# Expert weights loaded in 8 KB runs, with the gate and up products taken by quarters of the rows

## The chip, the cores and the metric

The kernel runs on one core of a Trainium2 chip. The metric is the device time of one launch in microseconds (us). Engines: PE (TensorE), DVE (VectorE), ACT (ScalarE), POOL (GpSimd), SP (SyncE, which here only issues DMAs).

## The reference

One layer of a hybrid backbone over 2048 tokens of 1024 channels. A first sub-layer (a projection, two state mixers, the product with `w_out`) takes the first 1100 us and more and is not touched, apart from its last stage. The second sub-layer is a mixture of 32 experts; each token goes to 2 of them:

```
x = x + g1 * rmsnorm(y, norm_post_mix)
h = rmsnorm(x, norm_pre_ffn) * (1.0 + sc2) + sh2        # the second norm
lg, le = h @ w_rg + b_rg, h @ w_re + b_re               # router: group, then 2 of its 8 experts
for each expert e, for each block of 128 of its (token, weight) pairs:
    xb  = h[tok]
    hid = silu(xb @ w_gate[e]) * (xb @ w_up[e])         # 1024 -> 512
    yb  = hid @ w_down[e]                               # 512 -> 1024
    out[tok] += yb * weight
x = x + g2 * rmsnorm(out, norm_post_ffn)
```

All is float32, and the products carry the float32 precision by splitting each operand into a high part (rounded to the PE's fp32r format) and a low part (the rest): high x high, high x low and low x high are added up.

## The kernel before

Stages follow each other: projection, mixers, **residual** (1111 to 1387 us of the trace), **experts** (1387 to about 2284) and the combining of the rows (to the end). Every engine runs its own program, written out by hand; semaphores tie them together.

**Residual.** It runs over 16 tiles of 128 tokens. For each, PE multiplies with `w_out`, DVE and ACT form the residual `r_x`, DVE forms the second norm `r_h` (also `h2`) in two operations (L2257 times the scale, L2259 plus the shift), PE transposes `r_h` (L2101) for the router's product, and a DMA stores it in DRAM (`second_norm`), where the experts' blocks gather their rows. The eight transposes take the channels k*128 to k*128+127, so the router's weights lie with channel k*128+p on partition p.

**Experts.** `over_blocks` loops over the experts and, within one, over its blocks (48 in all). The last block of an expert has `following`, the number of the next expert: in it the weights of the next expert are also converted. There are 31 such blocks. A block's body, by engine:

- PE: 48 gate and up products into `pG` (two halves of 256 gate and 256 up columns, in PSUM tile `r_py`; L2513 and L2514 high parts of x by both weight parts, L2517 the low part), two transposes of each half of the hidden rows (`turn_h`, L2501), eight transposes of the next block's rows (`turn_x`, L2494), and 24 products with w_down (L2522), 82 in all.
- ACT: silu of half 0 (L2578, into `e_sg`), the copy that makes the high parts of third 0 of the next weights (`high`, L2573: two operations, a sixth each), silu of half 1, the high part of `e_hT` (L2585) and `e_xT` (L2566), `high` of third 1, the output copy `e_y` (L2593, which waits until the scatter of the block before has left the buffer), `high` of third 2.
- DVE: `e_hid` (L2628) of each half, the low parts of `e_hT`, `e_xT` and of the weights (`low`, L2619, two operations a third, each behind its high sixth), its half of `e_y` (L2640).
- SP: loads `e_w_whole`, the raw weights, a third (2 MB) at a time; each third has one buffer, and its load waits until both low sixths of the same third of the expert before are made. Thirds 0 and 1 are columns 0 to 255 and 256 to 511 of w_gate and w_up, in runs of 256 floats (1 KB); third 2 is w_down in runs of 4 KB. So half h of the products needs third h only.
- POOL: gathers the rows of the next block (`e_x`) and scatters and adds the output of the block before (`rows_summed`, L2444), both through the DMA queue q0; the weight loads go through q1. Both carry rows of 1024 floats, one a packet.

`e_w_high` and `e_w_low` are single too: a sixth of the next expert may be written only when the products of this expert that read it are done. In third 0 that is when half 0's 24 products are (`prodG` of half 0).

## Time and profile before

| | |
|---|---|
| median of 3 runs | 2333.85 us (2333.26 to 2334.17) |
| the profiled execution | 2337.66 us, span 2336.0 us |
| experts' 48 blocks | 1386.8 to 2284.1 us |
| mean granted PE clock | 0.969 of full speed |
| DMA traffic | 518.11 MB, mean 222 GB/s |
| products on PE | 11618 instructions |

Busy times are shares of the whole span, over stages with different limits. What bounds the experts is read block by block: a block's length is the distance between the first gate product of one and of the next. In what follows "at 5.6" means 5.6 us after that first product, where a block is spoken of.

### The profile page before, as it was taken

What the parts mean: (1) busy time and instruction counts of PE and PEld (TensorE: products, weight loads), DVE (VectorE), ACT (ScalarE), POOL (GpSimd) and SP (SyncE); (2) the same over time, 40 slices, a digit from 0 to 9 for tenths busy, and PEclk for the clock granted to TensorE, in tenths of its full rate; (3) what the DMA queues carried; (4) which work ended last, traced back from release to release, by engine and by line L of the source; (5) the groups of instructions that cost most, each with busy time, mean ns of one, the idle gap of its engine ahead of it and who ended that gap; (6) DMA issues with size and microseconds to landing.
All of it is one profiled execution on the core that took longest, in us unless ns stands there. A gap on an engine that the chain in (4) does not pass through costs nothing. (4 is left out here: it accounts for less than half of the span.)

```text
span 2336.0 us, 35426 instructions
## 1 busy us (share of the span) xinstructions
PE 2177.8 (93%) x11618; PEld 1836.8 (79%) x11619; DVE 1400.3 (60%) x2033; ACT 1055.3 (45%) x1518; POOL 643.1 (28%) x648
## 2 busy tenths in 40 slices
PE   8999999999999679998999979999999999999990
PEld 5888888899999568887788858778788888887770
DVE  6322222377555578887566665765767675647776
ACT  4422332243223026665333234755666665547763
POOL 0000000000000558887222232221333333323333
PEclk9999999999999889999999989999999999999995
DMA  8632333546551987765554335998988887868997
GB/s 308 237 108 109 127 142 139 187 158 214 175 175 54 333 331 240 233 220 203 160 214 150 118 124 168 344 285 256 338 263 268 270 276 244 252 174 278 350 347 302
DMA packets 297436, 518.11 MB, mean 222 GB/s; under 512 B 33492, under 2 KB 206108, under 8 KB 292584
## 3 DMA queue, kind: packets, MB, share of 16 engines
q1 hardware_dynamic: 271000, 439.52, 55.1%
q0 software_dynamic: 17136, 43.92, 8.4%
q10 hardware_dynamic: 9216, 33.56, 3.5%
q8 instruction: 51, 0.84, 0.2%
q14 instruction: 33, 0.27, 0.0%
HBM read 397.28 MB, written 128.57 MB: 225 GB/s over the span
## 5 line engine op out<-in xcount | busy, mean ns | idle before, releaser
L2619 DVE TENSOR_TENSOR e_w_low<-e_w_whole,e_w_high 128x2048 fp32r<-128x2048 f32 x192 | 431.1, 2287 | 90.6 <-ACT e_w_high L2573 87.1
L2573 ACT ACTIVATE e_w_high<-e_w_whole 128x2048 fp32r<-128x2048 f32 x190 | 353.9, 1914 | 30.2 <-DMA e_w_whole<-in_moe_w_down_dram 18.5
L2513 PE MATMUL r_py<-e_w_high,e_xT 128*128 128x512 f32 x768 | 298.9, 389 | 1.2 <-ACT e_xT L2566 1.2
L2514 PE MATMUL r_py<-e_w_low,e_xT 128*128 128x512 f32 x768 | 298.8, 389 | 0.0
L897 PE MATMUL proj_acc<-w_high,hT_high 128*128 128x512 f32 x672 | 263.9, 393 | 0.3 <-DVE hT_low L1010 0.3
L897 PE MATMUL proj_acc<-w_low,hT_high 128*128 128x512 f32 x672 | 262.0, 390 | 0.0
L897 PE MATMUL proj_acc<-w_high,hT_low 128*128 128x512 f32 x672 | 261.7, 389 | 0.0
L2522 PE MATMUL r_py<-e_w_high,e_hT 128*128 128x512 f32 x768 | 226.7, 407 | 18.0 <-ACT e_hT L2585 17.9
L2517 PE MATMUL r_py<-e_w_high,e_xT 128*128 128x512 f32 x768 | 189.9, 389 | 0.0
L2522 PEld LDWEIGHTS r_py<-e_w_high,e_hT 128*128 128x128 f32 x768 | 138.6, 191 | 45.8 <-ACT e_hT L2585 20.6
L2513 PEld LDWEIGHTS r_py<-e_w_high,e_xT 128*128 128x128 f32 x768 | 144.2, 188 | 31.3 <-issue 1.4
L2517 PEld LDWEIGHTS r_py<-e_w_high,e_xT 128*128 128x128 f32 x768 | 144.2, 188 | 29.9
L2514 PEld LDWEIGHTS r_py<-e_w_low,e_xT 128*128 128x128 f32 x768 | 144.2, 188 | 29.9
L887 PE MATMUL proj_acc<-hT_high,w_high 128*128 128x256 f32 x576 | 164.4, 285 | 0.0
L887 PE MATMUL proj_acc<-hT_low,w_high 128*128 128x256 f32 x576 | 164.1, 285 | 0.0
L887 PE MATMUL proj_acc<-hT_high,w_low 128*128 128x256 f32 x576 | 164.0, 285 | 0.0
L1230 DVE SCALAR_TENSOR_TENSOR conv_out<-ch,cw,conv_out 128x258 f32<-128x258 f32 x288 | 119.4, 480 | 72.3 <-ACT conv_out L805 72.2
L897 PEld LDWEIGHTS proj_acc<-w_high,hT_high 128*128 128x128 f32 x672 | 126.5, 188 | 29.5 <-issue 3.5
L897 PEld LDWEIGHTS proj_acc<-w_high,hT_low 128*128 128x128 f32 x672 | 126.3, 188 | 26.5
L897 PEld LDWEIGHTS proj_acc<-w_low,hT_high 128*128 128x128 f32 x672 | 126.4, 188 | 24.9
L2049 PE MATMUL r_py<-r_w_high,r_yT 128*128 128x512 f32 x512 | 142.1, 394 | 0.0
L2423 POOL COPY e_rows_held<-e_rows_held 128x6 int32<-128x6 int32 x48 | 32.2, 672 | 360.6 <-issue 253.1
(311 smaller groups left out, 4196.2 us busy)
## 6 DMA issues: line engine op xcount, KB each, us to landing
e_w_whole<-in_moe_w_gate_dram SPq DMA_DIRECT2D x64, 1024.0 KB
e_w_whole<-in_moe_w_up_dram SPq DMA_DIRECT2D x64, 1024.0 KB
e_w_whole<-in_moe_w_down_dram SPq DMA_DIRECT2D x64, 1024.0 KB
by_token<-tok SPq DMA_DIRECT2D x32, 512.0 KB, 3.0
w_in_raw<-in_w_mod_dram SPq DMA_DIRECT2D x32, 512.0 KB, 4.4
m_tok<-by_token SPq DMA_DIRECT2D x16, 768.0 KB, 5.5
s_kv<-by_token SPq DMA_DIRECT2D x20, 512.0 KB, 5.9
modulated_high<-hT_high SPq DMA_DIRECT2D x9, 1024.0 KB, 3.9
```

The source lines that it names most:

```text
L887: m = nc.tensor.matmul(bank[:, b * 2 * P:(b + 1) * 2 * P], a[:, PLACE[c], k, w], h[:, s, k], start=(k == 0 and n == 0), stop=(k == KD - 1 ...
L897: m = nc.tensor.matmul(bank, h[:, s, k, span], (wh if high_ else wl)[:, PLACE[c], k], start=(k == 0 and n == 0), stop=(k == KD - 1 and n = ...
L1230: V.scalar_tensor_tensor(out=v[:, c], in0=chb[:, c, k:k + OUT], scalar=cw[:, k, c:c + 1], in1=v[:, c], op0=ALU.mult, op1=ALU.add).then_inc ...
L2049: m = nc.tensor.matmul(py[:, s, n], yT[:, s, part, k], with_[:, k, n * 512:(n + 1) * 512], start=(k == 0 and part == 0 and with_ is wh), s ...
L2423: nc.gpsimd.tensor_copy(held[:, 0:2], held[:, 1:3]).then_inc(held_on.sem, 1)
L2513: nc.tensor.matmul(pG[:, half], xT[:, 0, k], wh[:, half, w], start=(k == 0), stop=False)
L2514: nc.tensor.matmul(pG[:, half], xT[:, 0, k], wl[:, half, w], start=False, stop=False)
L2517: m = nc.tensor.matmul(pG[:, half], xT[:, 1, k], wh[:, half, k * 512:(k + 1) * 512], start=False, stop=(k == KD - 1))
L2522: m = nc.tensor.matmul(pY[:, n], hT[:, part, k], with_[:, 2, c0:c0 + 512], start=first, stop=last)
L2573: nc.scalar.activation(wh[:, third, part], raw[:, third, part], ACT.Copy).then_inc(whs.sem, 1)
L2619: nc.vector.tensor_tensor(wl[:, third, part], raw[:, third, part], wh[:, third, part].bitcast(F32), ALU.subtract).then_inc(wls.sem, 1)
```

## The change

1. **Loads.** Partition p now receives rows 8p to 8p+7 of w_gate and w_up, whole rows of 512 floats. Third 0 is the first four of these rows of both matrices, third 1 the last four: runs of four neighbouring rows, 8 KB. w_down stays as it was. The router's weights are loaded in the same order of rows.
2. **Second norm.** For the products to match, channel 8q+k of `r_h` is stored at position k*128+q. DVE's two operations (now L2264, L2266) run over 128 x 128 x 8 elements; the output (and the first input of the second) has a stride of 512 bytes between neighbouring elements.
3. **Converted weights.** `e_w_high` and `e_w_low` keep gate and up columns of a half side by side, so a sixth is written in runs of 256 floats (`sixth_of`), and read in whole.
4. **Products.** Both halves now need both thirds. PE takes the first four row chunks for both halves (24 products, then the new counter `rows_done`), then the last four for half 0 (12 products, `prodG` of half 0) and half 1 (12, `prodG` of half 1).
5. **Order on ACT and DVE.** In a block with `following`, ACT waits for third 0 of the next weights and for `rows_done`, makes the first high sixth, and only then silu of half 0; the second sixth stays between the silus. DVE makes the first low sixth ahead of `e_hid` of half 0.

```diff
+def by_chunks(v):
+    return v.rearrange("p (k q) -> p q k", k=KD)
+
+
+def by_rows(v):
+    return v.rearrange("p (q k) -> p q k", k=KD)
...
@@ residual: sync @@
-        sp.dma_start(wr[:, :, 0:NG], io["moe_w_rg"].rearrange("o (k p) n -> p (o k) n", p=P)).then_inc(one, 16)
+        sp.dma_start(wr[:, :, 0:NG], io["moe_w_rg"].rearrange("o (p k) n -> p (o k) n", k=KD)).then_inc(one, 16)
...
@@ residual: vector @@
-                nc.vector.scalar_tensor_tensor(out=h2[:, 1 - s], in0=x1[:, 1 - s], scalar=ss[:, 3:4], in1=g["mod"][:, 2], op0=ALU.mult, op1=ALU.mult).then_inc(h2m.sem, 1)
+                nc.vector.scalar_tensor_tensor(out=by_chunks(h2[:, 1 - s]), in0=by_rows(x1[:, 1 - s]), scalar=ss[:, 3:4], in1=by_rows(g["mod"][:, 2]), op0=ALU.mult, op1=ALU.mult).then_inc(h2m.sem, 1)
                 dve.wait_ge(h2m.sem, h2m.at(t - 1))
-                nc.vector.tensor_tensor(h2[:, 1 - s], h2[:, 1 - s], g["mod"][:, 1], ALU.add).then_inc(h2s.sem, 1)
+                nc.vector.tensor_tensor(by_chunks(h2[:, 1 - s]), by_chunks(h2[:, 1 - s]), by_rows(g["mod"][:, 1]), ALU.add).then_inc(h2s.sem, 1)
...
@@ load_sixth @@
     if third < 2:
-        to = raw[:, third].rearrange("p (k n f) -> p k n f", k=KD, n=2)[:, :, n]
-        eng.dma_start(to, io[src][0, bass.ds(e, 1), :, third * 256:(third + 1) * 256].rearrange("o (k p) f -> p (o k) f", p=P)).then_inc(landed, 16)
+        rows = KD // 2
+        to = raw[:, third, n * THIRD // 2:(n + 1) * THIRD // 2].rearrange("p (k f) -> p k f", k=rows)
+        eng.dma_start(to, io[src][0, bass.ds(e, 1)].rearrange("o (p k) f -> p (o k) f", k=KD)[:, third * rows:(third + 1) * rows]).then_inc(landed, 16)
...
+def sixth_of(buf, third, n, whole):
+
+    if third == 2 or whole:
+        part = buf[:, third, n * THIRD // 2:(n + 1) * THIRD // 2]
+        return part.rearrange("p (j f) -> p j f", f=256) if third < 2 else part
+    return buf[:, third].rearrange("p (j n f) -> p j n f", n=2, f=256)[:, :, n]
...
@@ experts: tensor, body @@
+            def gate_up(half, part, rows):
+                for k in range(4):
+                    w = slice((2 * k + half) * 512, (2 * k + half + 1) * 512)
+                    if part == 0:
+                        nc.tensor.matmul(pG[:, half], xT[:, 0, 4 * rows + k], wh[:, rows, w], start=(rows == 0 and k == 0), stop=False)
+                        nc.tensor.matmul(pG[:, half], xT[:, 0, 4 * rows + k], wl[:, rows, w], start=False, stop=False)
+                    else:
+                        m = nc.tensor.matmul(pG[:, half], xT[:, 1, 4 * rows + k], wh[:, rows, w], start=False, stop=(rows == 1 and k == 3))
+                        if k == 3:
+                            return m
+
+            pe.wait_ge(xTs.sem, xTs.at(b))
+            pe.wait_ge(wls.sem, wls.at(expert_of[0], 2))
             for half in range(2):
...
+                gate_up(half, 0, 0)
+            pe.wait_ge(xTl.sem, xTl.at(b))
+            for half in range(2):
+                m = gate_up(half, 1, 0)
+            m.then_inc(rows_done.sem, 1)
+            pe.wait_ge(wls.sem, wls.at(expert_of[0], 4))
+            for half in range(2):
+                gate_up(half, 0, 1)
+                gate_up(half, 1, 1).then_inc(prodG.sem, 1)
...
@@ experts: scalar, body @@
         def body(b, row, following):
+            if following is not None:
+                act.wait_ge(w_in.sem(0), w_in.at(following))
+                act.wait_ge(rows_done.sem, rows_done.at(b))
+                high_sixth(0, 0)
             for half in range(2):
                 act.wait_ge(prodG.sem, prodG.at(b, half + 1))
                 nc.scalar.activation(sg[:, half], pG[:, half, 0], ACT.Silu).then_inc(sgs.sem, 1)
                 if following is not None and half == 0:
-
-                    high(following, 0)
+                    high_sixth(0, 1)
...
@@ experts: vector, body @@
         def body(b, row, following):
+            if following is not None:
+                low_sixth(following, 0, 0)
             for half in range(2):
...
                 if following is not None and half == 0:
-                    low(following, 0)
+                    low_sixth(following, 0, 1)
```

ACT's program in a block with `following`, before the change, from the top of the body to the output copy (ISA and REGISTER_ALU rows carry waits and addresses; `e_sg` is the silu's output, `r_py` the PSUM tile of the products):

```order
L2578 ACT_TABLE_LOAD
L2578 ACTIVATE e_sg<-r_py 128x256
L2570 ISA
L2573 ACTIVATE e_w_high<-e_w_whole 128x2048 x2
L2577 REGISTER_ALU
L2578 ACTIVATE e_sg<-r_py 128x256
L2584 REGISTER_ALU
L2585 ACTIVATE e_hT<-r_pl 128x256
L2563 REGISTER_ALU
L2566 ACTIVATE e_xT<-r_pT 128x1024
```

The same place of ACT's program after the change:

```order
L2607 ISA
L2608 REGISTER_ALU
L2597 ACT_TABLE_LOAD
L2597 ACTIVATE e_w_high<-e_w_whole 128x8x256
L2611 ISA
L2612 ACT_TABLE_LOAD
L2612 ACTIVATE e_sg<-r_py 128x256
L2597 ACTIVATE e_w_high<-e_w_whole 128x8x256
L2611 REGISTER_ALU
L2612 ACTIVATE e_sg<-r_py 128x256
L2618 ACTIVATE e_hT<-r_pl 128x256
```

One of the two weight copies has moved ahead of the first silu, behind two waits, and there are two table loads in the body where there was one.

DVE's program at the same place, before the change:

```order
L2628 SCALAR_TENSOR_TENSOR e_hid<-e_sg,e_rows_held,r_py 128x256
L2618 ISA
L2619 TENSOR_TENSOR e_w_low<-e_w_whole,e_w_high 128x2048
L2618 REGISTER_ALU
L2619 TENSOR_TENSOR e_w_low<-e_w_whole,e_w_high 128x2048
L2623 REGISTER_ALU
```

And after it:

```order
L2648 ISA
L2649 TENSOR_TENSOR e_w_low<-e_w_whole,e_w_high 128x8x256
L2660 ISA
L2661 ISA
L2664 REGISTER_ALU
L2665 SCALAR_TENSOR_TENSOR e_hid<-e_sg,e_rows_held,r_py 128x256
L2648 REGISTER_ALU
L2649 TENSOR_TENSOR e_w_low<-e_w_whole,e_w_high 128x8x256
```

One subtraction of the next weights now stands ahead of `e_hid` of half 0.

## Rows read from the trace of the kernel before

**Rows 1.** The page: span, busy time of each engine, the two groups that convert weights
```profile
PE 2177.8 (93%) x11618; PEld 1836.8 (79%) x11619; DVE 1400.3 (60%) x2033; ACT 1055.3 (45%) x1518; POOL 643.1 (28%) x648
...
L2619 DVE TENSOR_TENSOR e_w_low<-e_w_whole,e_w_high 128x2048 fp32r<-128x2048 f32 x192 | 431.1, 2287 | 90.6 <-ACT e_w_high L2573 87.1
L2573 ACT ACTIVATE e_w_high<-e_w_whole 128x2048 fp32r<-128x2048 f32 x190 | 353.9, 1914 | 30.2 <-DMA e_w_whole<-in_moe_w_down_dram 18.5
```

**Rows 2.** Windows over stretches of blocks: stretch, length, busy times, PEclk, DMA share, GB/s
```profile
1464.30:1526.80 62.50, 54.94 (x253) 43.93 (x252) 49.41 (x37) 44.64 (x40) 17.75 (x15) 1.00 1.07 347
1526.80:1650.80 124.00, 124.00 (x590) 103.19 (x589) 78.40 (x67) 74.27 (x74) 33.23 (x35) 1.00 0.86 271
1650.80:1672.50 21.70, 19.49 (x85) 15.87 (x84) 16.71 (x13) 15.01 (x14) 6.78 (x5) 0.92 1.07 342
1672.50:2134.80 462.30, 461.65 (x2185) 382.91 (x2184) 290.09 (x247) 275.23 (x273) 144.71 (x130) 1.00 0.82 252
2134.80:2259.10 124.30, 112.28 (x506) 90.42 (x505) 99.66 (x73) 90.41 (x79) 42.48 (x30) 0.97 1.07 348
```

**Rows 3.** Waits over 1420 to 2295: engine, line, releaser, total, times, longest
```profile
ACT e_y L2593 <- DMA rows_summed<-e_y,e_rows_held: 61.0, 16, 6.7
...
ACT e_w_high L2573 <- DMA e_w_whole<-in_moe_w_down_dram: 18.5, 9, 3.1
PE r_py L2522 <- ACT e_hT L2585: 17.9, 10, 2.2
```

**Rows 4.** Timeline of POOL before the block that starts at 1650.8
```profile
1643.12 2.31 POOL L2444 DMA_INDIRECT rows_summed<-e_y,e_rows_held  x1 [0.38 <-issue]
```

**Rows 5.** Timeline of ACT in that block (start, duration, ..., idle before, releaser)
```profile
1653.67 0.60 ACT L2593 ACTIVATE e_y<-r_py 128x512 f32<-128x512 f32 x1 [2.36 <-DMA rows_summed<-e_y,e_rows_held]
1654.16 3.72 ACT L2573 ACTIVATE e_w_high<-e_w_whole 128x2048 fp32r<-128x2048 f32 x2
1657.90 1.28 ACT L2578 ACT_TABLE_LOAD   x1
...
1660.80 3.71 ACT L2573 ACTIVATE e_w_high<-e_w_whole 128x2048 fp32r<-128x2048 f32 x2 [1.22 <-DMA e_w_whole<-in_moe_w_up_dram]
1664.42 0.37 ACT L2578 ACTIVATE e_sg<-r_py 128x256 f32<-128x256 f32 x1
```

**Rows 6.** Timeline of PE in that block: the first products with w_down
```profile
1665.11 1.22 PE L2522 MATMUL r_py<-e_w_high,e_hT 128*128 128x512 f32 x2 [2.21 <-ACT e_hT L2585]
```

**Rows 7.** Windows of full DMA: a store in 8 KB runs, then loads in 4 KB runs
```profile
110.00:115.00 5.00, 5.00 (x25) 4.08 (x24) 0.00 (x0) 0.16 (x2) 0.00 (x0) 1.00 1.02 418
...
2300.00:2320.00 20.00, 0.00 (x0) 0.00 (x0) 20.00 (x19) 12.26 (x22) 13.57 (x13) 0.50 1.03 410
```

**Rows 8.** DMA queues over 1482 to 1484, both with work (q0: gather or scatter)
```profile
q0 software_dynamic: 74, 0.30, 75.6%
q1 hardware_dynamic: 75, 0.25, 33.6%
```

**Rows 9.** Timeline of ACT in an undisturbed block that starts at 1579.9
```profile
1585.57 0.38 ACT L2578 ACTIVATE e_sg<-r_py 128x256 f32<-128x256 f32 x1 [3.46 <-PE r_py L2517]
...
1591.02 0.38 ACT L2578 ACTIVATE e_sg<-r_py 128x256 f32<-128x256 f32 x1 [1.44 <-PE r_py L2517]
```

**Rows 10.** Timeline of DVE in the residual stage: the second norm's last operation
```profile
1330.08 1.23 DVE L2259 TENSOR_TENSOR r_h<-r_h,mod 128x1024 f32<-128x1024 f32 x1
```

**Rows 11.** Timeline of PE: its transposes of tile r_h, one tile and the last
```profile
1333.04 0.71 PE L2101 MATMUL r_pT<-ident,r_h 128*128 128x128 f32 x5
...
1357.21 0.98 PE L2101 MATMUL r_pT<-ident,r_h 128*128 128x128 f32 x7 [1.59 <-DVE r_h L2259]
```

**Rows 12.** Groups of small DVE operations by form: busy time, mean ns of one
```profile
L2235 DVE TENSOR_REDUCE o_sl<-o_wr 128x2 f32<-128x64 f32 x16 | 3.5, 220 | 0.5
L2206 DVE TENSOR_REDUCE o_s<-o_w 128x8 f32<-128x32 f32 x16 | 3.4, 211 | 0.5
...
L2193 DVE TENSOR_TENSOR o_l<-r_pl,r_br 128x4 f32<-128x4 f32 x16 | 2.5, 155 | 0.1
```

More of the change, by code:

```diff
@@ L2566, in xT_copy, with high_sixth @@
             nc.scalar.activation(xT[:, 0], pX[:], ACT.Copy).then_inc(xTs.sem, 1)
+        def high_sixth(third, n):
+            nc.scalar.activation(sixth_of(wh, third, n, False), sixth_of(raw, third, n, True), ACT.Copy).then_inc(whs.sem, 1)
         def high(e, third):
@@ L2571, in high @@
             for n in range(2):
-                part = slice(n * HALF, (n + 1) * HALF)
-                nc.scalar.activation(wh[:, third, part], raw[:, third, part], ACT.Copy).then_inc(whs.sem, 1)
+                high_sixth(third, n)
         def body(b, row, following):
+            if following is not None:
+                act.wait_ge(w_in.sem(0), w_in.at(following))
+                act.wait_ge(rows_done.sem, rows_done.at(b))
+                high_sixth(0, 0)
             for half in range(2):
```

25 lines of the change are left out of this document (8 added, 17 removed).

## The prediction

> **What bounds the kernel now.** I read the page first: PE is busy for 93% of the span, so it sets the time wherever nothing else is late [rows 1]. In the experts I then cut the trace at the first gate product of each block. The windows show two kinds. Seven undisturbed blocks take 124.0 us, 17.7 each, with PE busy throughout [rows 2]. Ten blocks take 62.5 (three), 21.7 (one) and 124.3 us (six), together 208.5 where 177 would do: 31.5 us lost. They are the blocks with `following` that come directly after another such block (experts of one block in a row), so that six thirds of weights, 12 MB, are wanted within two blocks. There the DMA share is 1.07 at 342 to 348 GB/s; in the calm ones it is 0.86 or 0.82 [rows 2]. In the 26 blocks from 1672.5 on, 462.3 us against 460.2, little is lost.
>
> The waits name what ends last in a lost stretch: PE's w_down products wait for ACT's high part of `e_hT`, 10 times, 17.9 us; behind that stands ACT, which has waited for the scatter of the previous output (61.0 us in 16 waits) and for the down third (18.5) [rows 3]. The block at 1650.8 shows the chain. POOL issued the scatter at 1643.12 [rows 4]; it lets ACT copy `e_y` only at 1653.67, frame 2.9 (us after the block's first product). Then come the high copy of the down third to 7.9, a table load of 1.28 us, silu 0, a wait for third 0 to 10.0, its two copies to 13.7, and silu 1 [rows 5]. `e_hT` follows, and PE starts down at 14.3 after 2.21 us idle [rows 6], where a calm block starts it at 11.9. So ACT's order and the DMA queue share the blame.
>
> **The loads: what they give.** The thirds of w_gate and w_up move at about 349 GB/s now, 2.10 MB in 6.0 us [rows 2]. A store in 8 KB runs ran at 418, loads in 4 KB runs at 410 [rows 7]. No row shows 8 KB loads; the bounds are 349 (nothing) and 418, and I take 410 to 418: 5.1 us. A run block's DMA sum was 2 x 6.0 + 5.1 for down + some 3.65 for gather and scatter = 20.8, which is the observed mean (20.85). It becomes 18.9. Upper bound of the gain: 10 x 2.0 = 20 us.
>
> The two queues share an engine packet by packet: while both had work, q0 sent 74 and q1 75 [rows 8]. Beside a 1 KB packet q0 therefore fared well; beside an 8 KB one it waits longer for each turn. An estimate: a 4 KB packet of q0 takes 75.6% of 2 us on 16 engines, over 74 packets, 327 ns [rows 8]; one of 8 KB at 418 GB/s takes 16 x 8192 B / 418 GB/s = 0.31 us. At a share of 1.07 a pair takes 0.59 us, and the scatter's 8 packets an engine 4.75 us instead of about 3.4. Bounds for the `e_y` copy: 0 to 1.3 us later. I take 0.7, since part of the scatter falls where q1 pauses.
>
> **ACT's new order.** A calm block is the measure: silus at 5.7 and 11.1 [rows 9], 24 products apart, 0.227 us each. Now `rows_done` comes with product 24 (5.6), `prodG` of half 0 with product 36 (8.4), of half 1 with 48 (11.1). ACT does high sixth 1.91 us, a second table load of 1.28 (the order shows two in every body with `following`), silu 0, the other sixth 1.91, silu 1; DVE 2.29 a sixth [rows 1].
> - Isolated following block (14): high 5.65 to 7.55, load to 8.85, silu 0 to 9.2, high to 11.1, silu 1 at 11.1; DVE's low 7.55 to 9.85, `e_hid`, low 11.1 to 13.35, `e_hid` 1 to 13.8, so the last low part of `e_hT` comes at 14.05 when PE wants it at 14.0. +0.1 each: +1.4. The cover is thin: whatever delays the first sixth by x costs x.
> - The first of a run (7), in which the down third's copies spill into the frame as well: +0.4 each, bounds 0 and 1.2: +2.8.
> - The second of a run (3; now 20.45 to 21.75, mean 21.0): `e_y` at 3.6, high of down 4.2 to 7.9, load to 9.2, first sixth to 11.1, second load to 12.4, silu 0, `e_hid` behind a low that ends at 13.4, hence `turn_h` at 13.8. But ACT's second sixth and silu 1 stand ahead of the `e_hT` copy, so down starts at about 15.3, against 14.3 before. Add 5.8 for 24 down products, and 1.2 for the slower clock after an idle PE (0.92 over this block now [rows 2]): 22.3. +1.3 each: +3.9.
> - Later ones of a run (7): if a block takes T, the next `e_y` copy moves by 11.7 - T against the start of the down third, and the block's silu by 20.6 - T. It settles at T = 20.4, ACT-bound, where DMA alone would allow 18.9. Now about 20.8. -0.4 each: -2.8.
>
> The wait for third 0 now stands ahead of silu 0, and with it everything behind it on ACT: both silus, `e_hT`, `e_xT`. It lands at 10.0 in the block shown [rows 5]; with loads 2 us quicker a block, at about 8.2, before ACT is free at 9.2. I cost it at nothing for that cover. SP's load of third 0 is issued about 1 us later, since the second low ends later (13.4 for 12.5); that lies within the same 1 us of room. Queued behind it on SP are only the loads of thirds 1 and 2.
>
> PE has the same 48 products; the waits for third 1's low now hold at product 25, as before, and the low part of x at product 17. Nothing. The write in runs of 256 floats is costed at nothing: each run is 1 KB long. Third 2's load, POOL's code, the combine stage: untouched.
>
> **The second norm.** The strided operations are not in the trace. The nearest rows: a reduction that reads 32 elements at a stride of 32 bytes takes 211 ns, one that reads 64 in a row 220, and an operation on 4 elements 155 [rows 12]. From the last two, 1.08 ns an element on top of 151; the strided one has 1.88. So +0.8 ns an element, 0.82 us an operation of 1024, 1.6 us a tile. In a middle tile L2259 ends at 1331.31 [rows 10] and PE's transposes start at 1333.04 [rows 11]: 1.73 us of room, which hides it. In the last tile they start at the operation's end [rows 11], so 1.6 us go to the path. Bounds: 0 (no penalty) and 2 or 3 times the element time.
>
> The Trainium skill bears on this (SBUF — State Buffer, Specifications): lines of 16 bytes, at least two accesses a line wanted for full bandwidth, a penalty at each new line. By it the 512-byte stride is slow for every element. The rows agree in direction (1.7 times), though at 32 bytes; how large it is at 512 no row here shows.
>
> **The sum**, against the profiled 2337.66: +1.4 +2.8 +3.9 -2.8 +1.6 = +6.9; one block of the 26 has already lost about 0.8 that shorter transfers return: +6.1, so 2343.8. The profiled run stands 3.8 us above the median of the runs (2333.85), so the forecast is **2340**.
>
> **The rivals.**
> - *A, the forecast:* ACT's order, the second table load and the later scatter eat the shorter transfers. Bounds of the terms: 2335 to 2346. Chance 0.43.
> - *B, faster:* the `e_y` copy comes earlier, not later, because the queue as a whole empties sooner (share falls below 1.0 between thirds). Then the run blocks follow the DMA sum: 208.5 to 188.5, -20; with +4.2, -0.8 and +1.6 that is -15: 2319, and 2314 if the first terms vanish. For it: 61.0 us of waits for the scatter [rows 3], a saturated queue in all ten blocks [rows 2]. Against: ACT's chain from `e_y` to `e_hT` is 11 us long without any wait. It decides where the `e_y` copy stands: at frame 2.0 or earlier B wins, from 3 on A. Chance 0.25.
> - *C:* A, and the strided operations take twice the element time or more: +1.1 us each, 2.2 a tile, 0.5 beyond the room in 12 tiles (6) and 2.2 in the last: +8.2 for +1.6, 2346.6; 2345 to 2353. Chance 0.17.
> - *D, the loads are no faster:* third 0 then lands at 10 to 11 and holds silu 0 back; 1.5 us more in ten blocks, +15 on A, 2355. Rows 7 speak against it. Chance 0.05.
> - *E, nothing to see:* B by half, 2330 to 2338. Chance 0.10.
>
> The Trainium skill (DMA: Bandwidth & Descriptors, Specifications) puts the least transfer for line rate at 512 B, by which 1 KB runs would already be at full rate and D would hold. The trace disagrees: 347 against 410 GB/s at a share above 1.0 in both [rows 2, 7].
>
> **How the numbers follow.** 0.2%, 4.7 us, is about what a measurement of this kernel can tell from no change: "same" reaches from 2329.2 to 2338.5. A puts about 0.14 below 2338.5 and 0.29 above. Faster: B and a bit of E, 0.27. Same: 0.14 of A, E's rest, a remainder: 0.25. Slower: A 0.29, C 0.17, D with what lies beyond: 0.48. The range has to take in most of B and C: 2314 to 2353; A's own is 2335 to 2346.
>
> **What would show it.** After: thirds 0 and 1 in run blocks at about 410 GB/s; two table loads in each following body; silu 0 at 8.9 in isolated following blocks and PE without a gap there; the second blocks of runs at about 22, later ones at about 20.4; PE's wait for `e_hT` larger in the second ones. L2264 and L2266 at about 2.1 us. Wrong if run blocks come near 19 (B), if the residual's period of a tile grows (C), if ACT waits for third 0 ahead of silu 0 (D), or if the PE idles in isolated following blocks, which I hold to be just covered: 14 blocks there turn each 0.3 us of mistake into 4.

## The result and the profile after

The changed kernel takes 2371.65 us (median of 4 runs, 2364.44 to 2381.62), the kernel before 2334.01 in the same comparison: a ratio of 1.0152, 95% interval 1.0123 to 1.0181. It is 36 us slower by that ratio (38 by the medians) where 6 were forecast, outside the range. Its runs also scatter over 17 us, those of before over 5. The profiled execution of the changed kernel (2381.62 us, span 2380.0) is the slowest of the four, so its stretches sum up to 44 us more than before, not to 36.

First the page of the changed kernel: busy times, then the two groups that convert weights.

```profile
PE 2198.4 (92%) x11618; PEld 1847.2 (78%) x11619; DVE 1426.0 (60%) x2033; ACT 1096.6 (46%) x1549; POOL 667.2 (28%) x648
...
L2649 DVE TENSOR_TENSOR e_w_low<-e_w_whole,e_w_high 128x2048 fp32r<-128x2048 f32 x192 | 433.4, 2288 | 164.1 <-ACT e_w_high L2597 164.1
L2597 ACT ACTIVATE e_w_high<-e_w_whole 128x2048 fp32r<-128x2048 f32 x190 | 357.0, 1915 | 32.1 <-PE r_py L2529 31.8
```

The durations of one operation are those of [rows 1] (2288 for 2287 ns, 1915 for 1914). Nothing has become slower by itself in these two; the time is in waiting. The first gate product of each block divides the experts again. The windows below are the run blocks of [rows 2] (three, one and six), two other blocks (1589.7 and 1744.3), and three microseconds in which only a load of gate and up ran (1732 to 1735):

```profile
1474.20:1536.30 62.10, 55.28 (x253) 43.87 (x252) 50.27 (x37) 49.40 (x43) 18.53 (x15) 1.00 1.00 358
...
1589.70:1607.60 17.90, 17.90 (x85) 14.65 (x84) 9.17 (x9) 12.52 (x12) 7.31 (x5) 1.00 0.60 212
1664.10:1690.50 26.40, 19.30 (x86) 16.00 (x85) 16.87 (x13) 16.36 (x15) 7.39 (x6) 0.87 0.85 282
1744.30:1768.00 23.70, 19.50 (x86) 15.89 (x85) 11.18 (x10) 8.35 (x10) 8.71 (x6) 0.93 0.83 269
1732.00:1735.00 3.00, 3.00 (x15) 2.47 (x14) 3.00 (x3) 2.98 (x2) 2.78 (x2) 1.00 1.02 429
2177.30:2302.10 124.80, 114.31 (x505) 92.54 (x504) 100.38 (x73) 98.39 (x85) 38.51 (x30) 0.95 0.96 344
```

What the reader is to see: the ten run blocks lose little more than before (62.1 for 62.5; 26.4 for 21.7; 124.8 for 124.3; together 213.3 for 208.5). But blocks that lost nothing before are now long. The one at 1744.3 takes 23.7 us; the one at 1589.7 still takes 17.9, but the block behind it 20.4. There are five such blocks (numbers 11, 18, 21, 24, 31, counted from 0). None of them has `following` itself; each comes directly behind one or two blocks that have. They were 17.7 us each before and now take 20.4, 23.7, 21.9, 22.8 and 22.1: 22.4 us lost in blocks that no step of the prediction speaks of. The DMA share is 0.83 to 1.00 in the slow stretches, where it was 1.07 in the run blocks before; and a load in 8 KB runs goes at 429 GB/s.

The waits over the experts, to be held against [rows 3]:

```profile
ACT e_y L2626 <- DMA rows_summed<-e_y,e_rows_held: 107.8, 26, 7.4
...
PE r_pl L2518 <- DVE e_hid L2665: 40.8, 14, 7.1
...
ACT L2597 <- DMA e_w_whole<-in_moe_w_up_dram: 10.0, 10, 1.8
```

ACT's output copy waits 107.8 us for the scatter in 26 places (61.0 in 16 before). PE now waits for the hidden rows. Number 17 and its successor show the whole chain. First POOL in the changed kernel, where block 17 starts at 1726.1, then in the kernel before, where it starts at 1707.9:

```profile
1732.05 2.28 POOL L2440 COPY e_rows_held<-e_rows_held 128x6 int32<-128x6 int32 x1 [9.57 <-issue]
1734.49 2.03 POOL L2445 COPY e_rows_held<-e_ids 128x3 int32<-128x3 int32 x1 [0.17 <-POOL e_rows_held L2440]
...
1738.27 2.97 POOL L2461 DMA_INDIRECT rows_summed<-e_y,e_rows_held  x1 [0.38 <-issue]
```

```profile
1712.88 1.15 POOL L2423 COPY e_rows_held<-e_rows_held 128x6 int32<-128x6 int32 x1 [8.60 <-issue]
1714.20 2.03 POOL L2428 COPY e_rows_held<-e_ids 128x3 int32<-128x3 int32 x1 [0.16 <-POOL e_rows_held L2423]
...
1717.97 2.32 POOL L2444 DMA_INDIRECT rows_summed<-e_y,e_rows_held  x1 [0.38 <-issue]
```

The scatter is issued at frame 12.2 instead of 10.1, and takes 2.97 us to be issued instead of 2.32. The first copy starts 1.0 us later in the block, and the two small copies together take 4.3 us (3.2 before); they take 0.2 us each where nothing holds them. Beside them, DVE of the changed kernel:

```profile
1729.80 6.68 DVE L2649 TENSOR_TENSOR e_w_low<-e_w_whole,e_w_high 128x2048 fp32r<-128x2048 f32 x3
```

Three subtractions in a row, 2.2 us apart, from 1729.80 to 1736.5. POOL's first copy ends at 1734.33, where the second of them ends; its second copy ends at 1736.52, with the third. The scatter's data then land so late that ACT, which may not overwrite `e_y` before, stands for 7.33 us. First ACT's copy in the kernel before, in block 18, which starts there at 1725.6; then ACT, DVE and PE in block 18 of the changed kernel, which starts at 1744.3:

```profile
1728.70 0.60 ACT L2593 ACTIVATE e_y<-r_py 128x512 f32<-128x512 f32 x1 [2.54 <-DMA rows_summed<-e_y,e_rows_held]
```

```profile
1752.04 0.60 ACT L2626 ACTIVATE e_y<-r_py 128x512 f32<-128x512 f32 x1 [7.33 <-DMA rows_summed<-e_y,e_rows_held]
1752.54 3.71 ACT L2597 ACTIVATE e_w_high<-e_w_whole 128x2048 fp32r<-128x2048 f32 x2
1756.26 1.28 ACT L2612 ACT_TABLE_LOAD   x1
1757.56 0.66 ACT L2612 ACTIVATE e_sg<-r_py 128x256 f32<-128x256 f32 x2
```

```profile
1758.89 0.87 DVE L2665 SCALAR_TENSOR_TENSOR e_hid<-e_sg,e_rows_held,r_py 128x256 f32<-128x256 f32 x2
```

```profile
1759.50 0.43 PE L2518 MATMUL r_pl<-ident,e_hid 128*128 128x128 f32 x2 [4.20 <-DVE e_hid L2665]
```

The output copy comes at frame 7.8 for 3.1 before. Behind it on ACT stand the two high sixths of the down third, a table load and the silus; DVE's hidden rows come behind its last low sixth; and PE, which wants them at the end of its 48 products, waits 4.20 us. At frame 3.1 the same row of work ended in time. In the five blocks the output copy comes 3.5 to 5.7 us later than before.

The packets' records of the two traces show where the time goes in block 17. The scatter is issued 2.1 us later and its issue takes 0.65 us longer; its 128 packets, of 327 ns each in both, are spread over 6.2 us instead of 3.9. What releases POOL's first copy stands in the kernel: POOL's loop waits until the scatter and the gather of the block before have landed. A late gather thus hands the lateness on. Before block 10, the gather lands 2.7 us later in its block than it did, POOL's first copy starts at frame 7.3 for 4.6, and the scatter is issued at 11.7 for 6.9.

Last, the second norm's two operations, and the two DMA queues in two microseconds of block 18 in which both had work:

```profile
L2264 DVE SCALAR_TENSOR_TENSOR r_h<-r_x,r_ss,mod 128x1024 f32<-128x1024 f32 x16 | 33.1, 2071 | 0.6 <-POOL r_ss L254 0.6
...
L2266 DVE TENSOR_TENSOR r_h<-r_h,mod 128x1024 f32<-128x1024 f32 x16 | 32.0, 2003 | 0.5
```

```profile
q0 software_dynamic: 53, 0.22, 55.1%
q1 hardware_dynamic: 50, 0.39, 50.9%
```

They take 2071 and 2003 ns, 0.79 and 0.78 us more than before. The queues still take turns packet by packet (53 to 50), as in [rows 8], and where a load in 8 KB runs is the neighbour each turn lets 8 KB of it pass ahead of 4 KB of q0.

### The profile page after: what moved, and what is told of

The parts are those of the page before. It is cut to its first block and busy times, and to the rows that moved or that the text cites. A ratio compares the mean times of both kernels' runs of the same rounds, so it can differ in the third digit from the quotient of the medians.

```text
span 2380.0 us, 35440 instructions
## 1 busy us (share of the span) xinstructions
PE 2198.4 (92%) x11618; PEld 1847.2 (78%) x11619; DVE 1426.0 (60%) x2033; ACT 1096.6 (46%) x1549; POOL 667.2 (28%) x648
## 5 line engine op out<-in xcount | busy, mean ns | idle before, releaser
L2649 DVE TENSOR_TENSOR e_w_low<-e_w_whole,e_w_high 128x2048 fp32r<-128x2048 f32 x192 | 433.4, 2288 | 164.1 <-ACT e_w_high L2597 164.1
L2597 ACT ACTIVATE e_w_high<-e_w_whole 128x2048 fp32r<-128x2048 f32 x190 | 357.0, 1915 | 32.1 <-PE r_py L2529 31.8
L2526 PE MATMUL r_py<-e_w_high,e_xT 128*128 128x512 f32 x768 | 298.9, 389 | 1.3 <-ACT e_xT L2594 1.3
L2529 PE MATMUL r_py<-e_w_high,e_xT 128*128 128x512 f32 x768 | 197.6, 389 | 0.0
L2440 POOL COPY e_rows_held<-e_rows_held 128x6 int32<-128x6 int32 x48 | 37.0, 772 | 385.5 <-issue 265.0
```

The source lines that it names most:

```text
L2440: nc.gpsimd.tensor_copy(held[:, 0:2], held[:, 1:3]).then_inc(held_on.sem, 1)
L2526: nc.tensor.matmul(pG[:, half], xT[:, 0, 4 * rows + k], wh[:, rows, w], start=(rows == 0 and k == 0), stop=False)
L2529: m = nc.tensor.matmul(pG[:, half], xT[:, 1, 4 * rows + k], wh[:, rows, w], start=False, stop=(rows == 1 and k == 3))
L2597: nc.scalar.activation(sixth_of(wh, third, n, False), sixth_of(raw, third, n, True), ACT.Copy).then_inc(whs.sem, 1)
L2649: nc.vector.tensor_tensor(sixth_of(wl, third, n, False), sixth_of(raw, third, n, True), sixth_of(wh, third, n, False).bitcast(F32), ALU.su ...
```

## The experiments

Fourteen kernels, each timed in five rounds against the kernel before. "Order" is the new order on ACT and DVE. Ratios are to the kernel before.

| kernel | median us | ratio, 95% interval |
|---|---|---|
| order_alone | 2359.93 | 1.0105 (1.0091 to 1.0120) |
| small_runs | 2356.16 | 1.0080 (1.0067 to 1.0093) |
| plain_norm | 2372.09 | 1.0172 (1.0140 to 1.0205) |
| early_scatter_after | 2443.65 | 1.0460 (1.0447 to 1.0474) |
| dve_rows_after | 2343.74 | 1.0028 (1.0019 to 1.0037) |
| dve_rows_before | 2332.35 | 0.9978 (0.9969 to 0.9987) |
| old_order | 2369.65 | 1.0155 (1.0139 to 1.0171) |
| strided_turn | 2378.69 | 1.0170 (1.0145 to 1.0195) |
| one_table | 2365.06 | 1.0119 (1.0101 to 1.0137) |
| all_edits | 2324.02 | 0.9948 (0.9935 to 0.9961) |
| all_edits_2k | 2325.77 | 0.9956 (0.9942 to 0.9970) |
| split_lows | 2366.61 | 1.0134 (1.0104 to 1.0164) |
| all_edits_1k | 2337.80 | 1.0000 (0.9991 to 1.0009) |
| order_rows | 2348.14 | 1.0044 (1.0030 to 1.0058) |

**order_alone: the order without the loads.** On the kernel before:

```diff
         def body(b, row, following):
+            if following is not None:
+                act.wait_ge(w_in.sem(0), w_in.at(following))
+                act.wait_ge(prodG.sem, prodG.at(b, 1))
+                high_sixth(0, 0)
...
-                    high(following, 0)
+                    high_sixth(0, 1)
```

and likewise on DVE, one low sixth ahead of the hidden rows.

> The kernel before (1 KB runs, products by halves, plain second norm) with the new order of ACT and DVE alone: the first high sixth ahead of silu 0, the first low sixth ahead of the hidden rows. Theory ORDER (three subtractions in a row on DVE hold up POOL's small copies, so the scatter is issued 2 us later and the output copy waits): most of the loss is here, 20 to 30 us slower than before, with the blocks after a pair of following blocks at 20 us or more. Theory PACKETS (the scatter's 4 KB packets wait behind 8 KB ones): at most 8 us slower, what the hand schedule gave (+1.4, +2.8, +3.9), and those blocks stay at 17.7.

Measured: 23 us slower, but not where the theory ORDER said. The five blocks (11, 18, 21, 24, 31) stay at 17.7; the first and second blocks of a run grow (the seven first ones take 136.3 us together for 125.3, the three second ones 68.6 for 63.0). The waits:

```profile
ACT L2576 <- DMA e_w_whole<-in_moe_w_up_dram: 32.2, 17, 3.2
...
ACT e_y L2599 <- DMA rows_summed<-e_y,e_rows_held: 4.4, 4, 1.4
```

ACT no longer waits for the scatter (4.4 us); it waits for third 0, 32.2 us in 17 places. In block 17 of that kernel:

```profile
1721.80 1.28 ACT L2576 ACT_TABLE_LOAD   x1 [1.01 <-DMA e_w_whole<-in_moe_w_up_dram]
1723.09 1.92 ACT L2576 ACTIVATE e_w_high<-e_w_whole 128x2048 fp32r<-128x2048 f32 x1
1725.02 1.28 ACT L2585 ACT_TABLE_LOAD   x1
```

Third 0 lands 5.5 us into the block, later than ACT would take it; then come a table load, a sixth, and the second table load, all ahead of silu 0. ACT had been free since 4.5. The prediction had costed this wait at nothing, since it put its landing in a run at 8.2 and ACT's readiness at 9.2; it had not looked at the first blocks of runs, and in this kernel ACT waits in the second and later ones too (23.7 of the 32.2 us). So in its time ORDER was right (20 to 30 us), in its mechanism wrong.

**small_runs: the change with 1 KB packets.**

```diff
-        to = raw[:, third, n * THIRD // 2:(n + 1) * THIRD // 2].rearrange("p (k f) -> p k f", k=rows)
-        eng.dma_start(to, ...rearrange("o (p k) f -> p (o k) f", k=KD)[:, third * rows:(third + 1) * rows])
+        to = sixth_of(raw, third, n, False)
+        eng.dma_start(to, ...rearrange("o (p k) (h f) -> p (o k h) f", k=KD, h=2)[:, 2 * third * rows:2 * (third + 1) * rows])
...
-    if third == 2 or whole:
+    if third == 2:
```

> The changed kernel, but the eight rows of a partition are written into the raw buffer in runs of 1 KB, so that the packets are as small as before; rows, products, order and the strided norm are those of the change. PACKETS: 2340 to 2348, the late output copies gone. ORDER: 2362 or more, or slower still, since the transfers lose their speed too. If both act: in between, near 2355.

Measured: 2356, "in between", 15 us faster than with 8 KB packets. Again the same two waits:

```profile
ACT L2597 <- DMA e_w_whole<-in_moe_w_up_dram: 31.5, 17, 3.0
...
ACT e_y L2626 <- DMA rows_summed<-e_y,e_rows_held: 10.5, 6, 4.8
```

With 1 KB packets third 0 is late (31.5 us) and the scatter is not (10.5). With 8 KB packets it is the other way round: 10.0 and 107.8. The long runs shorten the one wait and lengthen the other by more. The blocks show it too. With 1 KB packets, though POOL's copies and the order are those of the change, the five blocks are back at 17.7 us (22.3 us less in all), while the seven first blocks of runs take 5.5 us more. So it takes 8 KB packets to make the five blocks long.

**plain_norm and strided_turn: the strided operations.** plain_norm stores the second norm as before (the router's weights too; the expert products pair channels with other rows). strided_turn does the same and mends the products on PE:

```diff
-                m = nc.tensor.transpose(pX[:, k], xb[:, k * P:(k + 1) * P], ident)
+                m = nc.tensor.transpose(pX[:, k], xb[:].rearrange("p (q k) -> p k q", k=KD)[:, k], ident)
```

> The changed kernel with the second norm's two operations unstrided and the router's weights in the old order of rows (so the tokens go to the same experts; the expert products then pair channels with the wrong rows of the weights, values only). Both theories: the residual stage shortens by about 5 us (1391.7 to 1386.8 at the first gate product), the rest stays: 5 us faster than the changed kernel.

> The changed kernel with the second norm stored plainly, and PE's eight transposes of a block's rows reading every eighth channel instead (a stride of 32 bytes). If PE reads strided rows at its usual pace the 5 us of the residual stage come back (first gate product at 1386 to 1388 for 1391.7) and the rest stays: 5 us faster than the changed kernel. If a strided read doubles a transpose (0.27 to 0.5 us), 8 x 0.25 x 48 = up to 90 us slower.

Measured: neither is faster in the median (2372 and 2379, with runs from 2366 to 2392). The effect is seen inside the stage only: from PE's first transpose of `r_y` to the first gate product it takes 275.5 us before, 278.2 in the changed kernel, 275.5 in plain_norm and 276.3 in strided_turn. So the strided norm costs some 2.6 us; in all traces of this document the stage takes 277.5 to 278.6 us with it and 275.2 to 276.3 without. The rest of the 4.9 by which the experts begin later lies ahead of this stage, in code that is not touched: the stage starts anywhere between 1106.7 and 1113.5 us in these traces. In the experts more than this differs from trace to trace: the five blocks take 110.9 us in the trace of the changed kernel, 96.7 in plain_norm, 101.9 in strided_turn. PE's strided transposes take 300 ns on average in strided_turn against 285 for the plain ones of plain_norm, and 278 with the same stride in all_edits below; plain ones take 273 to 307 in the other traces. A stride of 32 bytes costs PE nothing that can be told from this spread.

**early_scatter_after: the scatter ahead of the second copy.**

```diff
             shift(b)
+            scatter(b)
             take(b)
...
             pool.dma_start(ids[:], dram["ids"][bass.ds(row, P), :]).then_inc(ids_in.sem(0), 16)
-            scatter(b)
```

> The changed kernel, but POOL issues the scatter directly behind its first small copy, ahead of the second copy and of the load of the next row numbers: about 4 us earlier in the block. ORDER: takes back more than the 2 us that the copies lose, so 25 us or more faster than the changed kernel, 2345 or less. PACKETS: the scatter still crawls at 6 us beside the 8 KB loads, but starts earlier: 10 to 20 us faster, 2350 to 2360. The output copies' waits for the scatter (107.8 us in the changed kernel) fall accordingly.

Measured: 72 us slower than the changed kernel. A clear miss; neither theory had this. The waits say why:

```profile
POOL e_x L2451 <- DMA e_ids<-tokens_sorted: 272.8, 41, 9.5
...
DVE e_hid L2665 <- POOL e_rows_held L2440: 67.9, 22, 5.0
```

The load of the next row numbers goes through the same queue q0 as the scatter, and now stands behind its 128 packets: POOL waits 272.8 us for it (90.5 in the changed kernel), the gather and the next block's first copy are late, and DVE's hidden rows wait for that copy (67.9 us).

**dve_rows_after and dve_rows_before: POOL's copies on DVE.** Both on top of their kernels:

```diff
 gpsimd:
-            shift(b)
-            take(b)
             pool.wait_ge(taken.sem, taken.at(b))
 vector, behind its half of the output copy:
+            nc.vector.tensor_copy(held[:, 0], held[:, 1]).then_inc(moved.sem, 1)
+            ...
+            nc.vector.tensor_copy(held[:, 1], held[:, 2]).then_inc(held_on.sem, 1)
+            ...
+            nc.vector.tensor_copy(held[:, 2], ids[:]).then_inc(taken.sem, 1)
```

> The changed kernel, but the three small copies of row numbers that POOL made ahead of each scatter are made by DVE, right behind its half of the output copy. Theory PORT (in the changed kernel a gather that lands 1.6 us later beside 8 KB packets pushes POOL's two copies into DVE's row of back-to-back subtractions, each copy ends only with a subtraction, and the scatter is issued 4 to 5 us later): the scatters are issued at frame 1 to 6, the blocks 11, 18, 21, 24 and 31 fall back to about 18, and 15 to 25 us of the loss go: 2345 to 2357. Rival SLOW PACKETS ALONE (the scatter crawls beside 8 KB packets wherever it stands): those blocks stay above 19.5, no more than 8 us gained.

> The same edit on the kernel before. PORT: output copies that wait for the scatter (61.0 us in 16 waits) come earlier; the ten run blocks are bound by DMA all the same, so 0 to 10 us faster than before, unless the 0.6 us of small copies on DVE, which is busy nearly throughout in following blocks, cost more. SLOW PACKETS ALONE: no change or slower by up to 10.

Measured: 28 us faster than the changed kernel, 1.0028 of the kernel before. Blocks 11, 18, 21, 24 and 31 are back at 17.7 us. POOL in block 17, which starts at 1714.4 there, and the two waits:

```profile
1720.80 0.58 POOL L2474 DMA_DIRECT2D e_ids<-tokens_sorted  x1 [10.01 <-issue]
1721.76 2.93 POOL L2462 DMA_INDIRECT rows_summed<-e_y,e_rows_held  x1 [0.38 <-issue]
```

```profile
ACT L2593 <- DMA e_w_whole<-in_moe_w_up_dram: 12.5, 10, 1.9
...
ACT e_y L2622 <- DMA rows_summed<-e_y,e_rows_held: 5.9, 4, 3.8
```

The scatter is issued at frame 7.4 for 12.2, though it still takes 2.93 us to issue and its packets still take turns with 8 KB ones. ACT's wait for it falls from 107.8 to 5.9 us. So slow packets alone do not make the loss; the late issue is needed. With small_runs this makes two conditions: take away the 8 KB packets or POOL's copies, and the five blocks are 17.7 us again. On the kernel before, the same edit brings some 5 us (0.9978).

**split_lows: shorter operations on DVE.**

```diff
-            nc.vector.tensor_tensor(low, raw, high, ALU.subtract).then_inc(wls.sem, 1)
+            nc.vector.tensor_tensor(low[half[0]], raw[half[0]], high[half[0]], ALU.subtract)
+            nc.vector.tensor_tensor(low[half[1]], raw[half[1]], high[half[1]], ALU.subtract).then_inc(wls.sem, 1)
```

> The changed kernel with each subtraction of weights on DVE cut in two halves, nothing else. PORT (a copy on POOL is held until the DVE operation running beside it ends): POOL's copies, up to 2.3 us long in the changed kernel, are now at most 1.2 us, the scatters are issued 1 to 2 us earlier, and 5 to 15 us of the loss come back although DVE has more instructions. If POOL's copies are slow for another reason, they stay at up to 2.3 us, and the time is that of the changed kernel or a few us more for 192 more operations.

Measured: 2366.6, 5 us faster than the changed kernel, less than the scatter of its runs (2360.6 to 2386.9): inconclusive as a time. Its trace tells more of the mechanism. Of POOL's 98 small copies, 31 took over 1.5 us in the changed kernel, here 5, as PORT had it. But three of the five took 4.83, 4.85 and 5.45 us. The first of them on POOL, then DVE beside it:

```profile
1645.75 4.83 POOL L2440 COPY e_rows_held<-e_rows_held 128x6 int32<-128x6 int32 x1 [9.57 <-issue]
1650.74 0.19 POOL L2445 COPY e_rows_held<-e_ids 128x3 int32<-128x3 int32 x1 [0.16 <-POOL e_rows_held L2440]
```

```profile
1645.90 1.22 DVE L2651 TENSOR_TENSOR e_w_low<-e_w_whole,e_w_high 128x1024 fp32r<-128x1024 f32 x1
...
1649.31 1.22 DVE L2652 TENSOR_TENSOR e_w_low<-e_w_whole,e_w_high 128x1024 fp32r<-128x1024 f32 x1
1650.61 0.48 DVE L2668 SCALAR_TENSOR_TENSOR e_hid<-e_sg,e_rows_held,r_py 128x256 f32<-128x256 f32 x1
```

The copy begins at 1645.75 and ends at 1650.58. DVE's operations follow one another without a gap until 1650.53, the end of one and four whole ones; the copy ends when DVE first pauses. The other two long ones end in the same way, behind four whole ones each. The next copy, a moment later, takes 0.19 us. So a small POOL operation does not always get its turn at the end of one DVE operation, it can wait for the whole row. The theory PORT as it was written (held until the operation beside it ends) was too narrow. Nor are held copies new: 27 of 98 took over 1.5 us before the change, and 28 in small_runs. What is new is that a scatter issued so late has to pass 8 KB packets.

How sharp this is shows when the traces of the five kernels with 8 KB runs, the new order and POOL's copies in their place are read together (the changed kernel, plain_norm, strided_turn, one_table below and split_lows). In each, 14 blocks with `following` stand ahead of one without; number 14, itself over 25 us long, is left out here. Where the scatter of the block is issued at frame 11.4 or earlier (46 times), the next block takes 17.7 to 18.0 us. Where it is issued at 11.7 or later (19 times), the next block takes 20.0 to 24.3, but for one of 17.9. What divides early from late is one subtraction of DVE. POOL's first copy, in blocks 20 and 23 of plain_norm, which start at 1774.7 and 1829.3:

```profile
1780.53 0.19 POOL L2440 COPY e_rows_held<-e_rows_held 128x6 int32<-128x6 int32 x1 [9.46 <-issue]
```

```profile
1835.21 2.29 POOL L2440 COPY e_rows_held<-e_rows_held 128x6 int32<-128x6 int32 x1 [9.56 <-issue]
```

It starts at frame 5.84 in the one and 5.91 in the other, beside a subtraction that ends at about 6.0. In block 20 it gets through with that end, in block 23 it is held for one more subtraction. POOL's second copy then ends at 8.2 and 10.4, the scatter is issued at 10.0 and 12.1, and the next block takes 17.7 and 23.4 us. In the changed kernel the first copy of blocks 17, 20 and 23 starts at 5.9 and goes the slow way in all three. The changed kernel has five late scatters in its trace, the others two to five. That runs differ by 17 us because the number of such blocks differs from execution to execution would follow from this; only one execution of each kernel was profiled, so it is not shown.

**old_order: 8 KB loads and quarters with the old order.**

```diff
-            if following is not None:
-                act.wait_ge(w_in.sem(0), w_in.at(following))
-                act.wait_ge(rows_done.sem, rows_done.at(b))
-                high_sixth(0, 0)
...
-                    high_sixth(0, 1)
+                    act.wait_ge(rows_done.sem, rows_done.at(b))
+                    high(following, 0)
```

and likewise on DVE, both low sixths behind the first hidden rows.

> The changed kernel (8 KB runs, products by quarters, strided norm), with the old order on ACT and DVE: both high sixths between the silus, both low ones between the two hidden rows. Silu 1 then comes at 12.6 for 11.1, the second hidden rows at 15.5 for 13.8, so PE should wait some 1.5 us in each of 31 following blocks, +40 us; against that no wait for third 0 ahead of silu 0 and one table load less. If the new order is what costs (ORDER), this is still faster than the changed kernel, below 2365; if the order is needed for the quarters, it is slower, 2385 or more.

Measured: 2369.7, between the two answers that were expected; as slow as the change, in another way. Every following block takes 19.6 us, no more and no less, the ten run blocks too (196.2 us together, the fewest but one):

```profile
PE r_py L2550 <- ACT e_hT L2615: 24.9, 31, 0.8
...
PE r_pr L2518 <- DVE e_hid L2660: 16.9, 31, 0.5
```

Two waits a block, of 0.8 and 0.5 us, 42 of the some 59 us in these 31 blocks; what makes up the rest was not looked for. With the old order the quarters cost every following block 1.9 us; the new order takes that away in the isolated ones and has its own price elsewhere.

**one_table: a silu of one column ahead of the wait.**

```diff
             if following is not None:
+                nc.scalar.activation(tiny[:], g["ident"][:, 0:1], ACT.Silu)
                 act.wait_ge(w_in.sem(0), w_in.at(following))
```

> The changed kernel with a silu of one column put at the top of ACT's body in following blocks, ahead of the wait for third 0: its table load stands ahead of that wait and the two later ones are gone. Theory TABLE (the load behind the wait and the one ahead of silu 0 are on the path wherever third 0 lands late): the isolated following blocks go from 17.95 to 17.7 (-0.25 x 14), the second blocks of runs lose up to 2.5 us each, 8 to 15 us faster in all. Rival: in the changed kernel ACT is held by the scatter before, so the loads are hidden: no more than 4 us.

Measured: 6.6 us faster in the median (2365.1), between the two answers, and not clear of the spread: the two intervals overlap. ACT's wait for the scatter is 127.6 us in that trace: as long as the scatter is late, a faster ACT waits longer for it.

**all_edits, all_edits_2k, all_edits_1k: the obstacles taken away together.** dve_rows_after, strided_turn and one_table in one kernel, then the same with runs of 2 KB and of 1 KB.

> The changed kernel with three edits together: the copies of row numbers on DVE, the second norm stored plainly with strided transposes on PE, and one table load. If the loss was the sum of these (late scatter 28 us, norm 5, tables 8 to 15), what is left of 2372 is 2324 to 2331, faster than the kernel before and than its version with the copies on DVE (2332). If something else of the new order costs (third 0 awaited ahead of silu 0), it stays at 2335 or above.

> The same with the rows of gate and up laid side by side in the raw buffer, so that the loads run in 2 KB pieces. If only the transfer's speed counts, it is 0 to 8 us slower than with 8 KB; if the gather and the scatter gain from smaller neighbours in the queue, it is as fast or faster.

> The version with all three edits (2324), with gate and up written in 1 KB runs. If the long runs bring what the run blocks' DMA sum said (18.9 for 20.8 a block, ten blocks), it is 10 to 20 us slower, 2334 to 2344; if the scatter's slower way beside long packets takes it all back, it is as fast, 2324 +- 4.

Measured: 2324.0, 0.9948 of the kernel before, at the lower end of what was expected, and 48 us faster than the changed kernel. The six run blocks at the end take 117.0 us for 124.3 [rows 2]:

```profile
2126.80:2243.80 117.00, 109.31 (x505) 89.38 (x504) 102.43 (x91) 92.37 (x85) 23.60 (x18) 0.99 1.01 370
```

ACT in the second block of that run, and the same waits as above:

```profile
2132.37 1.28 ACT L2604 ACT_TABLE_LOAD   x1
2133.67 0.20 ACT L2604 ACTIVATE e_tiny<-ident 128x1 f32<-128x1 f32 x1
2134.14 1.93 ACT L2594 ACTIVATE e_w_high<-e_w_whole 128x2048 fp32r<-128x2048 f32 x1 [0.27 <-DMA e_w_whole<-in_moe_w_up_dram]
2135.96 0.36 ACT L2610 ACTIVATE e_sg<-r_py 128x256 f32<-128x256 f32 x1
```

```profile
ACT e_y L2624 <- DMA rows_summed<-e_y,e_rows_held: 4.5, 7, 1.0
...
ACT e_w_high L2594 <- DMA e_w_whole<-in_moe_w_up_dram: 0.8, 2, 0.6
```

One table load, ahead of the wait; silu 0 directly behind the first sixth. The waits for the scatter (4.5) and for third 0 (0.8) are all but gone. Of the 14.9 us between this trace and that of the kernel before, 11.0 lie in the experts' 48 blocks; the rest lies ahead of the residual stage, where nothing was changed. 2 KB runs do as well (2325.8). With 1 KB runs the same kernel takes 2337.8, and its ten run blocks 210.0 us for 194.5: the long runs are worth 12 (by the ratios) to 14 us (by the medians), once nothing eats them.

**order_rows: the order alone, with POOL's copies on DVE.** order_alone and dve_rows_before in one kernel.

> The kernel before with the new order on ACT and DVE and the small copies on DVE. If POOL's held copies are the way in which the order costs, most of its 23 us vanish: 2336 to 2342 against 2332 for the copies on DVE alone. If it is the wait for third 0 ahead of silu 0 (1.0 us seen in the first blocks of runs, and more in the second ones) with the table loads behind it, 15 to 22 us stay: 2347 to 2355.

Measured: 2348.1, 16 us more than dve_rows_before. So 16 of the 23 us of the order stay when POOL makes no copies, and 7 go by them. What stays is the wait for third 0 (28.9 us of such waits in its trace) and the table loads behind it; the two were not told apart.

## Why the prediction was wrong

**What bounds the kernel** was read correctly: DMA sum and the chain from the output copy to `e_hid` and `e_hT` in run blocks. (Its first sentences say that the ten blocks come directly behind another with `following`. There are 17 of these; the ten that lost time have at least two ahead of them, as its later steps have it.) What it did not ask is what becomes of blocks that lose nothing now.

**The sum, term by term**, between the two profiled executions, in us:

| term | forecast | measured |
|---|---|---|
| isolated following blocks (14) | +1.4 | +2.7 |
| first blocks of runs (7) | +2.8 | +5.0 |
| second blocks of runs (3) | +3.9 | +7.7 |
| later blocks of runs (7) | -2.8 | -3.0 |
| second norm | +1.6 | +2.6 |
| one block that had lost time | -0.8 | in the first blocks |
| blocks 11, 18, 21, 24, 31 | nothing | +22.4 |
| block 0 | nothing | +3.4 |
| ahead of the residual stage | nothing | +2.3 |
| behind the experts | nothing | +0.9 |

Block 0 takes 19.3 to 30.2 us in these traces; why was not followed.

**The loads.** 8 KB at 410 to 418 was taken, 429 measured in one window. Right. Their worth was bounded at 20 us; all_edits against all_edits_1k shows 12 to 14. In the changed kernel itself they bring no gain but a loss of 15 us (against small_runs): their sign turns with what else is in the kernel.

**The step that failed** is the sentence "Bounds for the `e_y` copy: 0 to 1.3 us later. I take 0.7". It costed the scatter's packets only, and only in run blocks. The output copy came 3.5 to 5.7 us later in blocks 11, 18, 21, 24 and 31, which lie outside the runs, and 22.4 of the 44 us were lost there. Even the packets were costed too low: 128 of them were put at 4.75 us for 3.4, and in block 17 they took 6.2 for 3.9. The larger part, in that block 2.1 us of later issue and 0.65 of longer issue, lies with POOL, whose code was called untouched. Its two copies are held while DVE works on, and it starts them only when the gather of the block before has landed, later now. That the loss hangs on POOL's copies together with the long packets is shown by dve_rows_after (28 us back) and small_runs (15 us back), each with the five blocks at 17.7 again; that small operations are held while DVE works on is shown by the traces of block 17 and of split_lows. That the third subtraction in the row is needed for it is not shown: before the change DVE was busy beside the two copies as well (3.2 us for them). In order_alone and small_runs, with the new order, the copies of block 17 start at 3.8 and 4.1, end at 6.0 and 8.2, and the scatter is issued at 10.0. Why a POOL copy is held is not shown here; that both engines want the same path to memory fits, and the Trainium skill says so (SBUF — State Buffer, Terms: VectorE and GpSimd share a port pair, locked for a whole instruction, the loser blocked). The trace agrees with the blocking, and goes beyond it: 4.83 us over several instructions.

**The wait ahead of silu 0** was named, with its queue, and costed at nothing, since third 0 would land "at about 8.2, before ACT is free at 9.2". In the changed kernel it is 10.0 us in 10 waits, in three first blocks of runs and in seven of the ten behind them; with 1 KB packets it is 31.5 us, in all 17. So the cover that was counted on was not there in the run blocks either; with the faster loads the wait is small, with the slow ones it is most of what the order costs.

**Isolated following blocks:** 17.94 on average for 17.75, +0.2 where +0.1 was forecast. **First blocks of runs:** +0.7 each, within the bounds given. **Second blocks:** 20.6, 26.4 and 23.7 for 20.8, 21.8 and 20.4: +2.6 on average for +1.3. ACT's output copy comes at frame 7.9 in the longest of them (2.9 before), but at 1.9 and 2.7 in the other two, so the late scatter accounts for the one only. **Later blocks:** -0.4 each, as forecast, but by luck: they were to settle at 20.4, and in the last run they alternate (18.3, 23.3, 18.3, 22.7, 18.6).

**The second norm:** 0.82 us an operation forecast, 0.79 and 0.78 measured; 1.6 us on the path forecast, 2.6 measured.

**The rivals.** B (the scatter empties sooner) did not come. "It decides where the `e_y` copy stands" pointed to the right place, but no case had it at 7. C and D did not come: the strided operations stayed at 1.6 times their length, and the loads are faster. There was no rival in which blocks without `following` become slow, and these make half of the 44 us. The chances add up to 1, but "slower" got 0.48 where A's part, C and D make 0.51.

**What stays open:** how the 27 to 29 us by which long packets changed sign (+15 with POOL's copies in place, -12 to -14 without) divide between slower packets and later issue over all blocks; block 17 alone was taken apart. How much of the later issue comes by the gather, the row numbers and the held copies was not separated by a run.

## What to carry to other kernels

A faster bulk transfer is paid by whatever shares its queue engines: before lengthening packets, list the small transfers that others wait for, and look at how late each may be, in the calm stretches too. A wait that is moved ahead of a critical operation takes with it all that the engine must do behind it, table loads included; do such setup ahead of the wait. And reckon that a small GpSimd operation can take as long as VectorE's uninterrupted work beside it, and that what it issues comes later by as much.

## What the hardware showed unexpectedly

- A POOL copy of 128 x 6 elements takes 0.18 us alone, and up to 5.45 us beside a row of VectorE operations, ending when VectorE pauses.
- A POOL copy that starts 0.07 us later in its block (5.91 for 5.84, plain_norm) ends 2.2 us later, and with 8 KB packets in the other queue the next block takes 23.4 us for 17.7.
- The load of row numbers, issued on the same queue directly behind a scatter of 128 rows, kept POOL waiting 272.8 us over 41 blocks; ahead of the scatter 90.5.
- A VectorE operation that writes 1024 elements at a stride of 512 bytes takes 2.07 us for 1.28; PE's transposes that read at a stride of 32 bytes take 276 to 300 ns, unstrided ones 273 to 307.
- Loads in 2 KB runs were as good as in 8 KB (2325.8 and 2324.0); in 1 KB runs the kernel was 12 to 14 us slower.
